# Gate projections of a hybrid attention layer: eight block products against Strassen's seven

## The reference, cut to what matters

```python
h = _rmsnorm(x, g_pre)                      # 1024 tokens x 1024
proj = einsum('bsd,dn->bsn', h, w_in)       # all heads, and 2 x 1024 gate columns at the end
...                                         # stick-breaking attention -> o_sb, gated linear attention -> o_gla
y_sb  = (o_sb * silu(sb_z)) @ w_o_sb        # 512 -> 1024
y_gla = (rmsnorm(o_gla) * silu(gla_z)) @ w_o_gla
gates = sigmoid(gate_logits + b_gate)       # gate_logits: the last 2048 columns of proj
merged = gates[..., :1024] * y_sb + gates[..., 1024:] * y_gla
x = x + merged @ w_out
return _rmsnorm(x, g_final)
```

## Time and profile before

| what | value |
|---|---|
| median of three runs | 848.06 us (847.97 to 848.68) |
| the profiled execution | 848.23 us; its span from first to last instruction 846.5 us |
| merge stage from the end of the first two gate tiles to the last branch product | 512.64 to 752.0 us |
| output stage to the last matmul | 752.0 to 840.07 us |
| mean granted TensorE clock | 0.998 of full |

### The profile page before, as it was taken

One profiled execution on the slowest core, in us unless ns is written; L12 is line 12 of the kernel. 1 busy time (PEld: TensorE's weight loads), 2 busy tenths in 40 slices (PEclk: granted clock), 3 DMA queues, 4 the chain that ended last, 5 costly groups with the idle time before them and its releaser, 6 DMA issues.

```text
span 846.5 us, 11838 instructions
## 1 busy us (share of the span) xinstructions
PE 820.5 (97%) x4561; PEld 683.8 (81%) x4561; DVE 484.1 (57%) x676; ACT 355.3 (42%) x590; POOL 10.3 (1%) x16
## 2 busy tenths in 40 slices
PE   5999999999999999999999999999999999999996
PEld 4777787787878788889899888888888888878885
DVE  6539897988899798954655573123123032174332
ACT  7437565665757565563252351212212211152221
POOL 1000000000000000020000000000000000000000
PEclk9999999999999999999999999999999999999999
DMA  8100001000000000111110002111111111062221
GB/s 281 53 26 26 26 26 50 22 27 25 25 25 25 26 26 26 51 50 50 51 50 2 26 26 69 41 41 50 50 50 50 50 50 50 1 248 100 100 93 57
DMA packets 62379, 44.75 MB, mean 53 GB/s; under 512 B 2796, under 2 KB 56199, under 8 KB 62344
## 3 DMA queue, kind: packets, MB, share of 16 engines
q1 hardware_dynamic: 62290, 44.25, 17.4%
q10 hardware_dynamic: 54, 0.01, 0.0%
HBM read 40.06 MB, written 4.19 MB: 52 GB/s over the span
## 4 chain that ended last, share of the span: by engine, by line
PE 74%; DVE 17%; issue 5%; ACT 2%; DMA 1%; DVEq 1%; SPq 0%; ACTq 0%
PE pj L617 21%; PE pj L493 15%; DVE surv L1197 7%; PE ob L781 5%; PE ob L753 5%; PE sc L753 5%; PE sc L781 5%; PE pj L636 4%; PE pj L509 4%; DVE wt_lo L1244 3%; PE ob L584 2%; PE tr L594 2%; DVE w_lo L1121 2%; DVE k_lo L1146 1%; ACT beta L878 1%
## 5 line engine op out<-in xcount | busy, mean ns | idle before, releaser
L1121 DVE TENSOR_TENSOR w_lo<-w_raw,w_hi 128x1024 fp32r<-128x1024 f32 x47 | 57.4, 1222 | 139.6 <-ACT w_hi L819 139.5
L493 PE MATMUL pj<-h_hi,w_lo 128*128 128x512 f32 x336 | 134.2, 399 | 0.0
L493 PE MATMUL pj<-h_hi,w_hi 128*128 128x512 f32 x336 | 133.8, 398 | 0.0
L493 PE MATMUL pj<-h_lo,w_hi 128*128 128x512 f32 x336 | 133.6, 398 | 0.0
L617 PE MATMUL pj<-h_hi,w_hi 128*128 128x512 f32 x256 | 99.8, 390 | 0.0
L617 PE MATMUL pj<-h_lo,w_hi 128*128 128x512 f32 x256 | 99.7, 389 | 0.0
L617 PE MATMUL pj<-h_hi,w_lo 128*128 128x512 f32 x256 | 99.7, 389 | 0.0
L1197 DVE TENSOR_TENSOR_SCAN surv<-surv 128x128 f32<-128x128 f32 (+3 forms) x64 | 86.3, 1349 | 15.5 <-ACT beta L878 15.5
L973 ACT ACTIVATE gate<-pj,gate_bias 128x512 f32<-128x512 f32 x32 | 22.1, 690 | 134.1 <-PE pj L617 134.1
L819 ACT ACTIVATE w_hi<-w_raw 128x1024 fp32r<-128x1024 f32 x47 | 49.7, 1057 | 63.9 <-PE ob L753 63.5
L493 PEld LDWEIGHTS pj<-h_hi,w_lo 128*128 128x128 f32 x336 | 63.5, 189 | 12.2 <-issue 0.5
(11 more groups left out here) (216 smaller groups left out, 1563.9 us busy)
## 6 DMA issues: line engine op xcount, KB each, us to landing
w_raw<-in_w_in SPq DMA_DIRECT2D x44, 512.0 KB, 3.8
x_t<-in_x SPq DMA_DIRECT2D x8, 512.0 KB, 6.6
wout_raw<-in_w_out SPq DMA_DIRECT2D x8, 512.0 KB, 7.4
x_res<-in_x SPq DMA_DIRECT2D x8, 512.0 KB, 3.8
out_y<-y_out SPq DMA_DIRECT2D x16, 256.0 KB, 2.1
w_raw<-in_w_o_sb SPq DMA_DIRECT2D x8, 256.0 KB, 2.9
w_raw<-in_w_o_gla SPq DMA_DIRECT2D x8, 256.0 KB, 3.2
w_up<-in_w_alpha_up SPq DMA_DIRECT2D x8, 16.0 KB, 1.8
```

The lines of the kernel that those rows point to most:

```text
L493: mm = pe.matmul(pj[bank][:, :], (w_lo if p == 2 else w_hi)[:, slot, k, :], (h_lo if p == 1 else h_hi)[:, k, HALF * h:HALF * h + HALF], st ...
L1121: dve.tensor_tensor(w_lo[:, slot, :, :], w_raw[:, slot, :, :], w_hi[:, slot, :, :].bitcast(F32), ALU.subtract).then_inc(lo_done, 1)
```

## The change

For the seven channel tiles after the first, the gate projections of a pair of column tiles, one of gate A and one of gate B (2 column tiles x 2 halves of k, times 2 halves of k x 2 halves of the tokens), are computed as seven block products of 12 matmuls (`gate_block`) by Strassen's scheme in Winograd's form, where there were eight. Four of them need sums of blocks of `h` (`tt`, `tt4`; made once), three need sums of weight blocks (`weight_sums`, four DVE operations per tile). The products j = 0 to 6 go to banks 0, 1, 2, 3, 0, 2, 3 of a set of four, two sets alternating: the last three add to what stands in the bank after DVE or ACT has read it. DVE combines them by five additions per tile, each raising `comb`; ACT applies four sigmoids per tile on halves.

The branch products of all eight tiles come first, 32 banks of 12 matmuls. Those of tile 0 are merged at once; the other 28 banks are copied by ACT into a ring of two (`y_ring`) and stored by SP to the DRAM scratch `y_dram`. They are loaded back per tile into `y_back`, which has one slot. The gate weights of a tile are loaded to `graw`, also one slot: two transfers of 512 KB. `m_step` counts three steps per tile: the product with branch 0, and the two operations of `merge_b`.

On ACT, `high_item(v, j)` waits for the weights or their sums and for the product (v-1, j) that last read its buffer. In the output stage the channel tiles come in reverse order, `m_hi`/`m_lo` take the place of `w_hi`/`w_lo`, and `w_out` is loaded from the last gate tile on. Loops that ran over pairs of tiles are written out. The core of the diff:

```diff
+NP = 7
+PROD_BANK = (0, 1, 2, 3, 0, 2, 3)
+Y_PARTS = {31: ((1, 0), (2, 0)), 32: ((3, 0), (4, 0)), 33: ((5, 0), (6, 0)), 34: ((7, 0), (7, 1)),
+           35: ((1, 1), (2, 1)), 36: ((3, 1), (4, 1)), 37: ((5, 1), (6, 1))}
+Y_LAST = 37
+Y_SB_BANKS = 18
+Y_BANKS = 32
...
+        y_dram = nc.dram_tensor("y_scratch", (NP, 2, P, SEQ), F32, kind="Internal").ap()
...
+        gate_banks = [[pj[0][:, :], pj[1][:, :], tr[0][:, :], tr[1][:, :]], ring4]
...
+            def load_y(n):
+                sp.wait_ge(lo_done, n - 1)
+                parts = ((0, 0), (0, 1)) if n == 30 else Y_PARTS[n]
+                for side, loaded in enumerate((raw_loaded, half_loaded)):
+                    u, br = parts[side]
+                    sp.dma_start(w_raw[:, n % 2, 4 * side:4 * side + 4, :],
+                                 (wo_gla_v if br else wo_sb_v)[:, :, P * u:P * u + P]).then_inc(loaded[n % 2], 16)
+            def store_y(n):
+                for side, (u, br) in enumerate(Y_PARTS[n]):
+                    for h in range(2):
+                        c = 4 * (n - 31) + 2 * side + h
+                        sp.wait_ge(y_copied, c + 1)
+                        sp.dma_start(y_dram[u - 1, br][:, HALF * h:HALF * h + HALF], y_ring[:, c % 2, :])\
+                            .then_inc(y_stored[c % 2], 16)
+            def load_graw(v):
+                for g, col in enumerate((COL_GA, COL_GB)):
+                    sp.dma_start(graw[:, g, :, :], w_in_v[:, :, col + P * (v + 1):col + P * (v + 2)])\
+                        .then_inc(graw_loaded, 16)
+            def load_back(v):
+                for br in range(2):
+                    sp.dma_start(y_back[:, br, :], y_dram[v, br]).then_inc(back_loaded, 16)
+            for n in range(30, 33):
+                load_y(n)
+            for n in range(31, Y_LAST + 1):
+                if n + 2 <= Y_LAST:
+                    load_y(n + 2)
+                if n == 36:
+                    sp.wait_ge(t_lo, 12)
+                    load_graw(0)
+                store_y(n)
+            for parity in range(2):
+                sp.wait_ge(y_stored[parity], 16 * (Y_BANKS - 4) // 2)
+            sp.wait_ge(y_ready, Y_BANKS)
+            load_back(0)
+            for v in range(1, NP):
+                sp.wait_ge(item_lo, NP * v)
+                load_graw(v)
+                sp.wait_ge(m_step, 3 * v)
+                load_back(v)
             for c in range(KT):
                 e, kk = c // 4, 2 * (c % 4)
-                sp.dma_start(wout_raw[:, kk:kk + 2, e * HALF:(e + 1) * HALF],
-                             w_out_v[:, kk:kk + 2, e * HALF:(e + 1) * HALF]).then_inc(wout_loaded[c], 16)
+                sp.wait_ge(prod_done, NP * (NP - 1) + 2 + e)
+                sp.dma_start(wout_raw[e][:, kk:kk + 2, :], w_out_v[:, kk:kk + 2, e * HALF:(e + 1) * HALF])\
+                    .then_inc(wout_loaded[c], 16)
...
+            def y_products(c, slot, side, br, h):
+                for k in range(4):
+                    for p in range(3):
+                        mm = pe.matmul(ring4[c % 4], (w_lo if p == 2 else w_hi)[:, slot, 4 * side + k, :],
+                                       (g_lo if p == 1 else g_hi)[:, G_SLOT[4 * br + k], HALF * h:HALF * h + HALF],
+                                       start=(k == 0 and p == 0), stop=(k == 3 and p == 2))
+                mm.then_inc(y_ready, 1)
+            gate_tile(N4 + 1, (N4 + 1) % 2, 2)
+            pe.wait_ge(lo_done, 31)
+            for h in range(2):
+                for br in range(2):
+                    pe.wait_ge(gs_lo, 4 * br + 4)
+                    y_products(2 * h + br, 0, br, br, h)
+            for n, parts in Y_PARTS.items():
+                pe.wait_ge(lo_done, n + 1)
+                for side in range(2):
                     for h in range(2):
+                        c = 4 * (n - 30) + 2 * side + h
+                        if c < 8:
+                            pe.wait_ge(y0_free, c - 3)
+                        else:
+                            pe.wait_ge(y_copied, c - 7)
+                        y_products(c, n % 2, side, parts[side][1], h)
...
+            moving = [b11, (t2_op[0][:, :, :], t2_op[1][:, :, :]), t1_op, (t3_op[0][:, :, :], t3_op[1][:, :, :]), b21,
+                      b22, (t4_op[0][:, :, :], t4_op[1][:, :, :])]
...
+            def gate_block(v, j):
+                bank_of = gate_banks[v % 2][PROD_BANK[j]]
...
+                if v == 1 and j < 4:
+                    pe.wait_ge(y_copied, Y_BANKS - 4)
+                if v >= 2 and j == 0:
+                    pe.wait_ge(sig_a, 2 * (v - 2) + 1)
+                if v >= 2 and j in (1, 2, 3):
+                    pe.wait_ge(comb, 5 * (v - 2) + (1, 4, 5)[j - 1])
+                if j == 4:
+                    pe.wait_ge(p1_copied, v + 1)
+                if j in (5, 6):
+                    pe.wait_ge(comb, 5 * v + j - 3)
+                pe.wait_ge(item_lo, NP * v + j + 1)
+                for k in range(4):
+                    for p in range(3):
+                        mm = pe.matmul(bank_of, (gw_lo if p == 2 else gw_hi)[j][:, k, :], moving[j][p == 1][:, k, :],
+                                       start=(j < 4 and k == 0 and p == 0), stop=(k == 3 and p == 2),
+                                       skip_group_check=True)
+                mm.then_inc(prod_done, 1)
+            for v in range(NP):
+                for j in range(NP):
+                    gate_block(v, j)
...
+            for n in range(31, Y_LAST + 1):
+                if n < Y_LAST:
+                    y_high(n + 1, y_ready, 4 * (n - 30))
+                k = n - 31
+                copy_y(n, 0)
...
+            def finish_b(v):
+                act.wait_ge(comb, 5 * v + 5)
+                act.activation(gates2[:, 1, 0:HALF], gates2[:, 1, 0:HALF], ACT.Sigmoid,
+                               bias=cols[:, 17 + v:18 + v]).then_inc(sig_b, 1)
+            for v in range(NP):
+                if v == 0:
+                    for j in (2, 3, 4, 5):
+                        high_item(0, j)
+                high_item(v, 6)
+                if v:
+                    finish_b(v - 1)
+                act.wait_ge(prod_done, NP * v + 1)
+                if v:
+                    act.wait_ge(m_step, 3 * v - 2)
+                act.activation(gates2[:, 0, HALF:SEQ], gate_banks[v % 2][0], ACT.Copy).then_inc(p1_copied, 1)
+                if v + 1 < NP:
+                    for j in range(3):
+                        high_item(v + 1, j)
+                act.wait_ge(comb, 5 * v + 3)
+                act.activation(gates2[:, 1, HALF:SEQ], gates2[:, 1, HALF:SEQ], ACT.Sigmoid,
+                               bias=cols[:, 17 + v:18 + v]).then_inc(sig_b, 1)
+                if v + 1 < NP:
+                    high_item(v + 1, 3)
+                act.wait_ge(prod_done, NP * v + 5)
+                act.activation(gates2[:, 0, 0:HALF], gate_banks[v % 2][0], ACT.Sigmoid,
+                               bias=cols[:, 9 + v:10 + v]).then_inc(sig_a, 1)
+                if v + 1 < NP:
+                    high_item(v + 1, 4)
+                else:
+                    wout_high(0)
+                    wout_high(1)
+                act.wait_ge(comb, 5 * v + 4)
+                act.activation(gates2[:, 0, HALF:SEQ], gates2[:, 0, HALF:SEQ], ACT.Sigmoid,
+                               bias=cols[:, 9 + v:10 + v]).then_inc(sig_a, 1)
+                if v + 1 < NP:
+                    high_item(v + 1, 5)
...
+            def weight_sums(v):
+                dve.wait_ge(graw_loaded, 32 * v + 32)
+                if v:
+                    dve.wait_ge(item_lo, NP * v)
+                dve.tensor_tensor(s3t[:, :, :], a11, a21, ALU.subtract).then_inc(s_ready, 1)
+                dve.tensor_tensor(a21, a21, a22, ALU.add).then_inc(s_ready, 1)
+                dve.wait_ge(s_ready, 4 * v + 2)
+                dve.tensor_tensor(s2t[:, :, :], a21, a11, ALU.subtract).then_inc(s_ready, 1)
+                dve.wait_ge(s_ready, 4 * v + 3)
+                dve.tensor_tensor(s4t[:, :, :], a12, s2t[:, :, :], ALU.subtract).then_inc(s_ready, 1)
+            def low_item(v, j):
+                dve.wait_ge(item_hi, NP * v + j + 1)
+                dve.tensor_tensor(gw_lo[j][:, :, :], item_src[j], gw_hi[j][:, :, :].bitcast(F32), ALU.subtract)\
+                    .then_inc(item_lo, 1)
...
+            def last_block(v):
+                dve.wait_ge(prod_done, NP * v + 7)
+                dve.tensor_tensor(s_b1, s_b1, gate_banks[v % 2][3], ALU.add).then_inc(comb, 1)
+            def merge_b(v):
+                own = KT - 2 - v
+                dve.wait_ge(sig_b, 2 * v + 2)
+                dve.tensor_tensor(s_b, s_b, y_back[:, 1, :], ALU.mult).then_inc(m_step, 1)
+                dve.wait_ge(m_step, 3 * v + 2)
+                dve.tensor_tensor(mT[:, own, :], mT[:, own, :], s_b, ALU.add).then_inc(m_step, 1)
+            for v in range(NP):
+                banks = gate_banks[v % 2]
+                if v == 0:
+                    for j in (2, 3, 4, 5):
```

(103 more changed lines are left out.)

307 lines of the change are left out of this document (181 added, 126 removed).

## The result

| kernel | median, us | runs | ratio to before |
|---|---|---|---|
| before, beside these runs | 848.21 | 847.97 to 848.68 | 1 |
| after | 868.35 | 866.75 to 869.58 | 1.0236 (1.0217 to 1.0254) |

The changed kernel is slower by 20.1 us, and 11.9 us slower than the forecast. Its profiled execution took 867.86 us.

The account below looks back on a forecast made before the run. The prediction took the number of matmuls to bound the kernel before, and a load loop the gate stage after: -19.0 + 23.6 + 3.9 = +8.5 us, so 856.7 profiled and 856.5 median, range 848 to 867 us.

Parts of the forecast that it names:

- the loop: Gate stage: loads, sums, `comb`, sigmoids, `merge_b`, next loads close a loop without TensorE, 23.65 us per tile against TensorE's 19.04.
- TensorE stays the bound: Rival, gate stage: loop and loads fit in under about 21.7 us; in full, without gaps, 833 us; chance 0.10.
- Branch stage: From 512.64 us: TensorE needs 87.0 us, hiding the other engines' work, and the stage ends at 599.7 us.
- The ring of two: Rival, branch stage: slow stores make the ring bind; at 6 us a store, +17 us, 873; chance 0.03.
- The gate stage: 588 matmuls in some 157 us, cadence near 23.7 us, TensorE idle ahead of block 5; gaps sum to 23.6 us.
- Work from VectorE's first sum to SP's wait: Gate stage loop: VectorE and ScalarE operations from the weights' landing to SP's next wait being met, 15.87 us.
- Loads, 7.8 us: Gate stage loop: 1.15 to first byte, 2.6 for two `y_back` loads, 3.6 for two weight loads, 0.4 landing.
- The estimate by the Trainium skill: Gate stage loads: fixed 2.0 us and 436 GB/s give 6.8 us for four loads, gaps of 3.6 us each.
- The clock, the step that failed second: Gate stage: the forecast's sum held no cost for TensorE's clock falling in the gaps; only a rival did.
- My case: Whole kernel: the load loop with gaps ahead of block 5, by itself 851 to 862 us; chance 0.65.
- a rival with a chance of 0.12: Gate stage: the clock falls in the gaps and slows the two blocks behind; +2.4 x 5, 868 us; chance 0.12.
- The hand-over: After tile 6: gaps of 2.25 us before the output stage and 2.7 before its last k tile; net +3.9 us.

Follow-up runs that it names:

- e1: Changed kernel with SP loading the next tile's weights ahead of its wait for `m_step` and of `y_back`: 839.53 us, ratio 0.990.
- e4: Changed kernel with the next tile's weight sums and first three `high_item` moved behind `comb` 2 and 3 on VectorE and ScalarE: 848.74 us.
- e5: Changed kernel with SP still waiting for `m_step`, then issuing the weights first and `y_back` behind them: 850.94 us, ratio 1.0038.
- e3: Changed kernel with 12 idle matmuls added between blocks 4 and 5 of tiles 1 to 5: 868.11 us, ratio 1.0227.
- e7: e6_both with an eighth block of 12 matmuls per tile, whose result is overwritten: 854.11 us, ratio 1.0072.
- e6_both: Changed kernel with the edits of both e1 and e4: 834.48 us, ratio 0.9844.
- e2: Changed kernel loading back only half of the tokens (2 KB rows) into `y_back` from tile 1 on: 866.0 us, ratio 1.0204.
- e9: Changed kernel loading back only half of the partitions (4 KB rows) into `y_back` from tile 1 on: 867.59 us, ratio 1.0219.
- e10: Changed kernel with 24 idle matmuls added between blocks 4 and 5 of tiles 1 to 5: 864.52 us, ratio 1.0208.

## Why the prediction was right in kind and too low

**Direction and mechanism.** Right, and shown: the loop closed by SP's order and the one slot of `y_back` (e1, e4 and e5 open or shorten it at three places; a second slot for `y_back` was not tried), TensorE not in it (e3), gaps ahead of block 5 put down to `comb` 2, the saving whole (e7). "TensorE stays the bound" (833) happened not in this kernel, but in e6_both, at 834.5.

**Branch stage.** Right. 384 matmuls from 512.03 to 599.07 us without a gap; the forecast had 599.7. The ring of two doesn't bind.

**The gate stage.** Forecast 133.3 + 23.6 = 156.9 us, measured from 598.9 to 764.3 = 165.4. The gaps themselves fit: from the end of a block at full pace to the next start 1.79, 6.59, 3.41, 3.60, 2.70 and 5.02, together 23.1. That is a coincidence of two errors. Turns of 24.62 us would have left gaps of 5.6 us, 29.7 in all with tile 0; the blocks took 9.0 us more than at full pace, and 6.6 of these came out of the gaps. By the loop the account is:
- Work from VectorE's first sum to SP's wait: 15.87 forecast, 15.95 to 16.1 measured. Right; +0.4 in five turns, and +0.2 where block 5 at the lower clock holds up `comb` 4.
- *Loads, 7.8 us, the step that failed first.* SP's issue to the first sum took 9.8, 8.2, 8.3, 8.6 and 8.2, 8.6 in the mean: +4.1 us in all. By e5 the two weight loads alone take 5.7 us, where the terms without `y_back` give 1.15 + 3.6 + 0.4 = 5.15; and `y_back` ahead of them costs 2.9 where the forecast had 2.6 for its bytes. That this second term came out near is luck: it isn't bytes over a rate, for halving the bytes changed a turn by 0.1 us at most (e2, e9). Why the first turn takes 9.8, no run shows; it does so in e2, e9 and e10 too (9.0, 9.7, 9.1). The estimate by the Trainium skill ("DMA: Bandwidth & Descriptors"), 6.8 us, was further off than the one from rows; the page fits it to transfers issued from GpSimd, and SP issues these.
- Tile 0: gap 1.79 instead of 0.5, and its blocks 0.1 longer: +1.4.
- *The clock, the step that failed second.* My case had it at nothing; a rival with a chance of 0.12 had 2.4 us in each of five gaps. Neither is right: in tiles 1 to 3 the loop takes the slower blocks up (but for the 0.2 above, 5.50 us for the 12 matmuls before `comb` 4 in tile 3), in tile 4 the clock doesn't fall, and in tile 5 all of it is on the path, +2.5. That the rival's number, 868 us, is the measured one is luck: its 12 us were to come from the clock alone, with the loads at 7.8.

**The hand-over.** The two gaps are 2.4 and 3.3 us, against 2.25 and 2.7: +0.8. Behind the second the clock is low again, 27 matmuls at 8.03 instead of 6.12: +1.9. The third output block starts at 783.24, 18.9 us behind the gate stage, where the forecast's terms give 15.8: +3.1, the last 0.4 being ends of matmuls that the timeline counts as busy, and rounding. Nobody's case had the clock here.

**The sum.** 856.7 - 0.6 (start) + 4.1 + 0.4 + 0.2 + 1.4 + 2.5 + 3.1 = 867.8; the profiled execution took 867.86. The mis-sized terms are thus the loads (+4.1) and the clock (+2.5 and +1.9), and e10, in which the clock didn't fall in this stage, had a median 3.8 us lower. The range ended at 867 because it held each error by itself, not the two together.

## What to carry to other kernels

When work is moved and its results come back through a buffer of one slot, write down the loop of loads, waits and lists that this closes; the busy times said that VectorE and ScalarE had room of some 25 us per tile, and the kernel lost by a wait in the wrong place on the engine that only issues transfers.
## What the runs showed of the hardware

- The second of the two weight loads landed 5.3 to 5.4 us after its issue with nothing issued ahead of it (e5), 6.9 to 8.5 (after) and, with half the bytes ahead, 6.2 to 8.2 (e2 and e9) behind two others issued 0.9 to 1.3 us before the first of them. The size of what stood ahead mattered by 0.5 us at most in the mean, that it stood there by some 2.
- The length of a gap didn't decide by itself whether TensorE's clock fell to 1.2 GHz. Idle times of TensorE by its timeline: in after 2.39 and 2.54 us left it at 2.4 GHz, while 3.25, 3.33, 3.44, 4.86 and 6.43 brought it down. In e3_fill 3.20 left it up, and it fell at gaps of 2.26, 2.60, 2.11 and 2.39. In e5_weights_first it fell at gaps of 2.38, 2.39, one of 2.42 and 1.95, and stayed up behind 2.46 and another 2.42. The shortest that it fell behind was 1.87 (e2_half_back). What decides is open. The lower level lasted 3.4 or 6.8 us each time before the end of the matmuls, and it could begin after TensorE had started again (e5: gap ended at 657.34, low from 658.8 to 662.2).
- Adding 120 idle matmuls, 27 us of TensorE's time, did not lengthen the kernel (its median was 3.8 us lower), since they lay in its gaps.
